# A two-layer decoder step on one core: another order of the matmul passes, the first two weight tiles together, a moved store, small copies on another engine

## The reference

```python
for i in range(2):
    x = x + mixer_i(rmsnorm(x, norm_mix[i]))          # 0: attention, 1: recurrent block
    x = x + conv_ffn(rmsnorm(x, norm_ffn[i]))
def conv_ffn(xn):                                     # buf: the last rows of the step before
    g, u = split(xn @ w_up)
    return (silu(causal_dwconv(g, buf, w, b)) * u) @ w_down
def recurrent_mixer(xn):
    xr, gate_in = split(xn @ w_in)
    xc = causal_dwconv(xr, conv_buf, conv_w, conv_b)  # width 4
    r, gi = sigmoid(block_diag(xc, w_a)), sigmoid(block_diag(xc, w_i))
    a = exp(-8 * r * softplus(-lam))
    h_t = a_t * h_(t-1) + sqrt(1 - a_t^2) * (gi_t * xc_t)
    return (h * gelu(gate_in)) @ w_out                # and the last h and conv rows as outputs
```

## Time and profile before

| | us |
|---|---|
| median of 3 executions | 1921.45 (1920.43 to 1925.03) |
| the profiled execution | 1921.14 |
| its span, first to last instruction | 1919.3 |

### The profile page before, as it was taken

The page is one execution under the profiler, slowest core; times in us unless marked ns, Lnnn a source line. Parts: engine busy times, 40 slices in busy tenths (PEclk is TensorE's granted clock), DMA queues, the critical chain, the costliest instruction groups (busy, mean ns, idle before and its releaser), DMA issues.

```text
span 1919.3 us, 35303 instructions
## 1 busy us (share of the span) xinstructions
PE 1881.5 (98%) x13021; PEld 1811.1 (94%) x13021; DVE 1106.1 (58%) x1966; ACT 901.5 (47%) x1842; POOL 797.3 (42%) x798
## 2 busy tenths in 40 slices
PE   7999999999999999999999999999989999999998
PEld 7986679999999999999999999999989999999998
DVE  3677755565556555545644645649863564564464
ACT  4455655554555455344333424356654342333333
POOL 3340013432223224253563473475535347347335
PEclk9999999999999999999999999999999999999999
DMA  5320101211111110223232233232222233223223
GB/s 151 67 57 2 26 17 44 82 32 48 35 38 32 48 36 16 72 78 88 78 99 77 88 89 88 80 107 77 67 74 74 81 88 89 86 79 99 77 82 98
DMA packets 253092, 131.62 MB, mean 69 GB/s; under 512 B 43073, under 2 KB 250754, under 8 KB 252882
## 3 DMA queue, kind: packets, MB, share of 16 engines
q1 hardware_dynamic: 252514, 128.56, 24.0%
q10 hardware_dynamic: 444, 1.29, 0.2%
HBM read 126.21 MB, written 3.61 MB: 68 GB/s over the span
## 4 chain that ended last, share of the span: by engine, by line
PE 91%; DVE 5%; ACT 2%; DMA 1%; issue 1%; POOL 0%; SPq 0%; DVEq 0%; ACTq 0%; POOLq 0%
PE ps L227 14%; PE ps L234 13%; PE ps L228 13%; PE ps L1232 7%; PE ps L1230 7%; PE ps L1231 7%; PE ps L1869 5%; PE ps L1867 5%; PE ps L1873 5%; PE ps L1260 3%; PE ps L1006 2%; PE ps L1197 2%; PE ps L240 1%; PE ps L1033 1%; PE ps L201 1%; PE ps L202 1%
## 5 line engine op out<-in xcount | busy, mean ns | idle before, releaser
L227 PE MATMUL ps<-split,whi 128*128 128x288 f32 x2128 | 578.9, 300 | 11.9 <-DVE split L281 5.3
L228 PE MATMUL ps<-split,whi 128*128 128x288 f32 x2128 | 575.9, 297 | 0.0
L195 POOL TENSOR_TENSOR wlo<-raw,whi 128x1024 fp32r<-128x1024 f32 x143 | 346.9, 2430 | 400.9 <-ACT whi L172 381.6
L227 PEld LDWEIGHTS ps<-split,whi 128*128 128x128 f32 x2128 | 402.7, 189 | 15.2 <-issue 10.9
L228 PEld LDWEIGHTS ps<-split,whi 128*128 128x128 f32 x2128 | 402.1, 189 | 0.4
L234 PE MATMUL ps<-split,wlo 128*128 128x288 f32 x2128 | 305.5, 295 | 0.0
L234 PEld LDWEIGHTS ps<-split,wlo 128*128 128x128 f32 x2128 | 290.4, 188 | 0.0
L1230 PE MATMUL ps<-split,split 128*128 128x384 f32 x768 | 268.2, 349 | 0.0
L1480 DVE TENSOR_REDUCE ssq<-arena 128x16 f32<-128x1024 f32 x128 | 156.1, 1220 | 186.6 <-ACT arena L1342 186.6
L1342 ACT ACTIVATE arena<-ps 128x384 f32<-128x384 f32 (+1 forms) x384 | 174.6, 456 | 184.6 <-PE ps L1232 181.5
L1232 PE MATMUL ps<-split,split 128*128 128x384 f32 x768 | 257.9, 336 | 0.0
(11 more groups left out here) (336 smaller groups left out, 3317.2 us busy)
## 6 DMA issues: line engine op xcount, KB each, us to landing
raw<-in_ffn_w_up SPq DMA_DIRECT2D x96, 512.0 KB, 3.7
raw<-in_ffn_w_down SPq DMA_DIRECT2D x48, 512.0 KB, 4.0
arena<-in_cache_ckv SPq DMA_DIRECT2D x128, 128.0 KB, 2.0
raw<-in_rec_w_in SPq DMA_DIRECT2D x16, 512.0 KB, 3.9
raw<-in_attn_w_o SPq DMA_DIRECT2D x8, 512.0 KB, 5.3
raw<-in_rec_w_out SPq DMA_DIRECT2D x8, 512.0 KB, 4.3
raw<-in_attn_w_down SPq DMA_DIRECT2D x7, 512.0 KB, 7.6
raw<-in_attn_w_uq SPq DMA_DIRECT2D x48, 64.0 KB, 2.2
```

The costliest lines, as they stand in the source:

```text
L195: pool.tensor_tensor(wlo[:, t % RING, :], raw[:, t % RING, :], f32(whi[:, t % RING, :]), ALU.subtract).then_inc(w_lo, 1)
L227: pe.matmul(o, wh[:, at + k, :], h, start=k == 0, stop=False)
L228: pe.matmul(o, wh[:, at + k, :], l, start=False, stop=False)
```

## The change

Six edits. (1) `tile_product` now runs block by block with all three passes (`product`), one half of the columns after the other (both halves together where activations still arrive or only some blocks are taken), and waits for the low weights before its first matmul. It serves the down and query projections and both feed-forwards. The old order lives on in `low_last_product`, used by the recurrent block and its output projection, there also one half after the other. (2) The first two tiles run together in `first_tiles`: high x high for both tiles chunk by chunk as the high chunks come, then low weights, then low activations; ScalarE casts tile 1 ahead of the activations. (3) In the prompt attention the first `key_norm` stands one unit later. (4) The recurrent block's copies of the last conv columns move to ScalarE, and those of the last states behind the scans, ahead of the joins. (5) There, GpSimd makes each low weight part in two instructions of 512. (6) `rec_store` stands after the load of O6 instead of O3.

```diff
+        def split_lo_twice(pool, t):
+            pool.wait_ge(w_hi, t + 1)
+            for c in (slice(0, 512), slice(512, 1024)):
+                ins = pool.tensor_tensor(wlo[:, t % RING, c], raw[:, t % RING, c], f32(whi[:, t % RING, c]), ALU.subtract)
+            ins.then_inc(w_lo, 1)
...
-        def tile_product(pe, t, a, xh, xl, it=0, at=0, kn=8, ready=None, part=None, out=None, low=None):
+        def tile_product(pe, t, a, xh, xl, it=0, at=0, kn=8, ready=None, part=None):
             if t:
-                pe.wait_ge(w_hi, t + 1 + 4 * it)
-            if a >= 2 and out is None:
+                pe.wait_ge(w_lo, t + 1 + 4 * it)
+            if a >= 2:
                 pe.wait_ge(acc_free[a % 2], a // 2 + 2 * it)
...
+            both = ready or kn < 8 or part
+            for h in (slice(0, 2),) if both else (slice(0, 1), slice(1, 2)):
+                for k in part or range(kn):
+                    if ready:
+                        ready(k)
+                    mm = product(pe, acc(a % 2)[h], wh[:, at + k, :], wl[:, at + k, :],
+                                 halves(xh[:, k, :])[h], halves(xl[:, k, :])[h], k == 0, k == kn - 1)
+            return mm
...
+        def first_tiles(pe):
...
+            pe.wait_ge(w_hi, 2)
+            for k in range(DC):
+                pe.wait_ge(n_hi, k + 1)
+                for t in range(2):
+                    for o, h in zip(acc(t), halves(xn_hi[:, k, :])):
+                        pe.matmul(o, wh[t][:, k, :], h, start=k == 0, stop=False)
+                if k == 3:
+                    input_sums(pe)
+            for t in range(2):
+                for k in range(DC):
...
+                    for o, h in zip(acc(t), halves(xn_hi[:, k, :])):
+                        pe.matmul(o, wl[t][:, k, :], h, start=False, stop=False)
+            for t in range(2):
+                for k in range(DC):
+                    pe.wait_ge(n_lo, k + 1)
+                    for o, l in zip(acc(t), halves(xn_lo[:, k, :])):
+                        mm = pe.matmul(o, wh[t][:, k, :], l, start=False, stop=k == DC - 1)
+                mm.then_inc(w_used, 1)
...
-                    if u % 8 == 4 and h // 2 < 7:
+                    if (u == 5 or u % 8 == 4 and u > 4) and h // 2 < 7:
                         key_norm(dve, h // 2 + 1)
...
                     act.activation(xcv[:, n % 2, 0:XC], xrb[:, n % 2, 0:XC], ACT.Identity,
                                    bias=rpar[:, n, R_CB:R_CB + 1], scale=rpar[:, n, R_CW:R_CW + 1]).then_inc(r_c1, 1)
+                    act.copy(hl[:, n, 1 + NB:1 + NB + XP], xrb[:, n % 2, TP:XW])
+                    act.copy(hl[:, n, 1 + NB + XP:HL].rearrange("p (w b) -> p b w", b=NB),
...
             dve.tensor_tensor_scan(m, a, v, 0.0, ALU.mult, ALU.add).then_inc(r_sc, 1)
+
+        def rec_states(dve, n):
+            m = mm_[n % 2]
             dve.wait_ge(r_sc, n + 1)
             dve.tensor_copy(hl[:, n, 0:1], m[:, TP - 1:TP])
...
             for d in range(DC):
                 load_tile(sp, OUT0 + d, out(d))
-                if d == 3:
+                if d == 6:
                     rec_store(sp)
...
             split_hi(act, 0)
+            split_hi(act, 1)
             act.wait_ge(rp_ev, 1)
             act.wait_ge(xt_ev, XTOK)
             for c in range(DC):
                 norm_high(act, 0, c)
-                if c == 4:
-                    split_hi(act, 1)
```

More of the change, by code:

```diff
@@ L220, in tile_product @@
             wl = wlo[:, t % RING, :].rearrange("p (k n) -> p k n", n=P)
-            out = out or acc(a % 2)
-            ks = part or range(kn)
-            for k in ks:
-                if ready:
-                    ready(k)
-                for o, h, l in zip(out, halves(xh[:, k, :]), halves(xl[:, k, :])):
-                    pe.matmul(o, wh[:, at + k, :], h, start=k == 0, stop=False)
-                    pe.matmul(o, wh[:, at + k, :], l, start=False, stop=False)
-            low = ks if low is None else low
@@ L230, in tile_product @@
-            if t and low:
-                pe.wait_ge(w_lo, t + 1 + 4 * it)
-            for k in low:
-                for o, h in zip(out, halves(xh[:, k, :])):
-                    mm = pe.matmul(o, wl[:, at + k, :], h, start=False, stop=k == kn - 1)
+            both = ready or kn < 8 or part
[5 more added lines that the diff above has]
+                                 halves(xh[:, k, :])[h], halves(xl[:, k, :])[h], k == 0, k == kn - 1)
@@ new lines, in tile_product, with low_last_product @@
+            return mm
+        def low_last_product(pe, t, a, xh, xl, ready=None, part=range(8), out=None, low=None):
+            pe.wait_ge(w_hi, t + 1)
+            if out is None:
+                pe.wait_ge(acc_free[a % 2], a // 2)
+            wh = whi[:, t % RING, :].rearrange("p (k n) -> p k n", n=P)
+            wl = wlo[:, t % RING, :].rearrange("p (k n) -> p k n", n=P)
+            out = out or acc(a % 2)
+            turns = (slice(0, 2),) if ready else (slice(0, 1), slice(1, 2))
+            for g in turns:
+                for k in part:
+                    if ready:
+                        ready(k)
+                    for o, h, l in zip(out[g], halves(xh[:, k, :])[g], halves(xl[:, k, :])[g]):
+                        pe.matmul(o, wh[:, k, :], h, start=k == 0, stop=False)
+                        pe.matmul(o, wh[:, k, :], l, start=False, stop=False)
+            low = part if low is None else low
+            if low:
+                pe.wait_ge(w_lo, t + 1)
+            for g in turns:
+                for k in low:
+                    for o, h in zip(out[g], halves(xh[:, k, :])[g]):
+                        mm = pe.matmul(o, wl[:, k, :], h, start=False, stop=k == 7)
@@ L2625, in rec_dve @@
                     rec_input(dve, n - 1)
+            for m in range(DC - 2, DC):
+                rec_states(dve, m)
             dve.wait_ge(r_yl, DC - 2)
```

50 lines of the change are left out of this document (25 added, 25 removed).

## The result

The changed kernel takes **1903.51 us** (median of four runs, 1903.01 to 1903.54), the kernel before 1921.56 in the same series. The ratio is 0.9902, with a 95% interval of 0.9885 to 0.9920: some 18 us faster. The forecast was 1912 with a range of 1907 to 1917.

What follows compares the result with a forecast made beforehand. TensorE, busy 98% of the span, was taken to bound the kernel. Gains of 2.9 (start) + 5.0 (store) + 1.3 (prompt attention) + 0 + 0 = 9.2 us off 1921.14 gave 1911.9, stated as 1912, range 1907 to 1917.

Steps and rivals of the forecast that it cites:

- The start: First two tiles: first product at about 18.1 us, tile 2 at 34.3 instead of 37.2; gain 2.9 us, bounds 2 and 5.
- The store: Output projection: O4's load no longer held behind the states' store, wait and low clock gone; gain 5.0 us, bounds 3.3 to 5.2.
- The prompt attention: Unit 5's maximum taken inside VectorE's wait for the key root; gain 1.3 us, bounds 0 and 4.0.
- the rival that has the next maximum late instead: Part of "Gains are given back": prompt loop gains nothing; whole case 1915.5 to 1918 us, chance 0.11.
- The pass order: About 5,100 matmuls, nearly all one half at a time: same pace as the old order, gain 0, bound 4.2 us.
- the 24-matmul pair: 24 matmuls of one half, block by block, at 133.3 ns each in the earlier trace; argued against a faster new order.
- what the rival had: "The new order is also faster": single half runs at 132.5 ns, 4.2 us more gain, 1907 to 1909.5 us; chance 0.15.
- The recurrent block: Moved copies and halved GpSimd low parts taken as gain 0, bounds -4.6 and +3 us.
- So neither the copies nor the halves bring the taps forward: Recurrent block: VectorE finishes at the sum of its and GpSimd's times, taps ending at 1348.1 against 1347.5 read.
- The bound of -4.6: Recurrent block, best case: all three TensorE waits gone, 1.5 + 0.8 + 2.3 us.
- The rival that opens the block: Recurrent block: pieces let VectorE's first scan through, two of three waits (about 3 us) go, 1907 to 1910 us; chance 0.08.
- The slower rival: Recurrent block: halved low parts add VectorE waits and length, up to 24 us on the path; slower or nearly so, chance 0.06.

Runs made afterwards that it cites:

- whole pieces: Changed kernel with GpSimd's low parts in the recurrent block in one instruction of 1024 columns again: 1904.19 us.
- three edits alone: Kernel before plus only the two tiles together at the start, the key norm one unit later and the store moved: 1911.48 us, ratio 0.9942.
- block undone: Changed kernel with all three recurrent-block edits (column and state copies, halved low parts) taken back, new pass order kept: 1905.88 us.
- other columns with the halves in turn: Changed kernel with both halves in turn, passes together, second half reading from columns 0, 64, 32 or 144: 6.320 us a tile, 6.347 from 144.

## Why the prediction was right or wrong

**The start** was right in mechanism and size. Tile 2 was put at 34.3 and came at 35.23. Of the 0.9 us of error 0.65 is in the sums: 2.35 us (22.13 to 24.48) where I let 1.7 stand, because the half clock lasted past 24 and not until 23.4. In the profiled executions of the kernels that have this start, tile 2 begins between 33.7 and 35.5, 34.3 on average. Part of the spread is the clock's. In the execution with the state copies put back the clock (third number from the right) reads

```profile
18.00:20.00 2.00, 2.00 (x12) 1.84 (x11) 2.00 (x2) 2.00 (x4) 2.00 (x2) 0.75 1.16 243
20.00:22.00 2.00, 2.00 (x11) 2.00 (x10) 2.00 (x2) 2.00 (x4) 1.01 (x1) 0.50 0.15 10
22.00:24.00 2.00, 2.00 (x14) 1.81 (x13) 2.00 (x4) 1.06 (x4) 0.00 (x0) 0.90 0.08 9
```

while the changed kernel's profiled execution stands at 0.50 from 18 to 24. Of the 1.4 us between these two, 0.4 are there before the first product (17.71 against 18.15), and 1.0 is the low clock's, which in the one was over before 24 and in the other was not.

**The store** was right: 5.1 against 5.0, wait and low clock both gone.

**The prompt attention** was right in mechanism, and its term was mis-sized: 2.7 against 1.3. I counted the 1.64 us that unit 5's maximum no longer waits for, less 0.3, and left the low clock behind the wait standing, though I had priced it (3.96 x 0.41 = 1.6) for the upper bound. In the traces the waits give 2.36 - 0.21 - 0.69 = 1.46, close to the 1.3, and the other 1.3 of the measured 2.7 is the clock's. The new 0.69 is a small part of the rival that has the next maximum late instead. At the store I had taken the clock's part into the term; here the same step was left out.

**The pass order** was wrong. "... the 24-matmul pair is the very order, and stands at 133.3" is the step that failed. The order was the same, but that pair (the second half of an attention output tile) reads another array, whose chunks are 288 columns long, so their starts alternate between two offsets 128 bytes apart. In the feed-forward each half has one offset for all its chunks. That this is why the pair stood at 133.3 is not shown: the mean of 131.6 and 133.4 would be 132.5, so the cause of the pair's pace stays open. What is shown is that its pace did not carry over: in the feed-forward the order takes 6.36 us a tile. The gain is about what the rival had, 4.2 (4.4 by the stretches, 3.9 by those of the kernel with the old order back), and its mechanism is not the rival's: half of the matmuls run at 131.6 and half stay at 133.4. The weights' wait at the start of a third cost nothing, as forecast.

**The recurrent block** was wrong. "So neither the copies nor the halves bring the taps forward" rests on one group, in which VectorE's time and GpSimd's added up. Over all eight groups the copies held VectorE for 11.7 us, of which 8.6 came back as a wait and 3.1 did not, and each of the three edits taken back costs the block 0.9 to 2.0 us. The bound of -4.6 held the 3.4, the value taken did not: I read VectorE's blocking where it was complete and took it for the rule. The rival that opens the block had two of the three waits of the earlier trace rows go; what went is the one of 0.8 us and parts of the others (2.3 to 1.8, 1.5 to 0.9), 1.9 us in all; the rest of the 3.4 is in smaller pieces. The slower rival had no part: with the halves the block is 1.4 us shorter than with whole pieces.

**The range.** Three of the four errors went the same way (4.4, 3.4 and 1.4 us against the start's 0.9), and two rivals that I had set as alternatives came true together; 1912 - 4.2 - 3 gives 1904.8, already below the range. The range covered one rival at a time.

## What to carry to other kernels

Read a pace together with the operands it was read on: before an order of matmuls is judged by a stretch elsewhere in the trace, see that the arrays start at the same offsets there, or run the order at the place where it is to stand. On the chain of an engine whose instructions wait for another engine's, as VectorE's do for GpSimd's here, count small instructions at the mean that their group shows (1.00 us for three columns) and not at what they take alone (0.17), and look at what the engine will wait for in their place: 8.6 of the copies' 11.7 us came back as another wait. Where a wait is removed, take the low clock behind it into the sum as well. When several rivals can hold at once, let the range reach to their sum.

## What was not expected of the hardware

**A matmul's pace hangs on where its columns start.** With one half at a time, 288-column matmuls start every 131.5 to 131.7 ns from an offset of 0 within 256 bytes, every 132.2 from 64 and every 133.4 from 128, offsets counted from the first half's start. The Trainium skill ("TensorE: Matmul & The Clock Gate", Wait — 56ns, not 53.3ns?) has, for matmuls back to back, the columns' time at 2.4 GHz plus a fixed 2.5 ns or so. By that it would be an estimated 120 + 2.5 = 122.5 ns here, whatever the offset; the fastest tiles of these traces (6.24 us) stand at 130.0, so for these operands the measurement decides. With both halves in turn the offsets count otherwise: a second half at 128 costs nothing (6.320 us a tile from 32 and from 288), and one at 64 slows all 48 matmuls to 132.2. Why the offset matters is open.

**One loop can have several paces.** The same tile in the same order took 6.24, 6.32 or 6.45 us, the same in a second execution, and two fulfilled waits ahead of the loop turned 6.24 into 6.45. With both halves read from the same column, both odd values were gone. The kernel before shows it in small: its tiles take 6.393 us in layer 1's first third and 6.400 in the other five. What chooses the pace is open.

**A wait may or may not cost the clock, and the clock may or may not cost time.** In the recurrent block, TensorE's wait ahead of the last group's gates is 2.2 to 3.0 us in six of the profiled executions. In four of them (three edits alone, whole pieces, state copies back, block undone) the clock fell to half behind it, as here with the state copies back,

```profile
1386.00:1389.00 3.00, 2.35 (x13) 2.35 (x14) 2.82 (x6) 2.97 (x4) 0.82 (x1) 0.79 0.04 12
1389.00:1391.00 2.00, 2.00 (x11) 2.00 (x10) 1.97 (x6) 1.06 (x2) 0.00 (x0) 0.50 0.00 0
```

and in two (the kernel before, the column copies on VectorE) it did not. Of the eight executions where that wait is 1.8 us, the clock fell in two (other columns with the halves in turn, and the old order back). There the block ended only 0.3 us later than without, 136.78 against 136.49 to 136.58: behind it TensorE stands for VectorE once more, in the changed kernel for 0.9 us, and in these two that wait was gone. So most of what the half clock cost here was paid for out of the wait behind it.
